# Splitting layer 1's first adaLN group around layer 0's experts, and writing a group's columns ahead of the gating

## The chip, the cores and the metric

The kernel runs on one core of a Trainium2 chip. What counts is the device time of one execution in microseconds (us); the kernel before took 1294.08 us, the median of three runs between 1293.26 and 1298.45.

## What is computed

One inference step of a four-layer diffusion backbone, float32 throughout: 128 context tokens and 256 latent tokens of width 1024 (384 columns together). Cut to what matters here:

```python
for i in range(4):                      # mixer: pool, mLSTM, MLA, pool
    mod = silu(cvec) @ w_ada[i] + b_ada[i]        # 6 x 1024 values, for each of two condition vectors
    h = rmsnorm(x, norm_mix[i]) * (1 + mod[1]) + mod[0]
    x = x + mod[2] * mixer(h)
    h = rmsnorm(x, norm_ffn[i]) * (1 + mod[4]) + mod[3]
    x = x + mod[5] * moe(h, ...)        # 16 experts of 256, two a token
```

w_ada of a layer is 1024 x 6144: 24 MB of weights for two vectors, so each byte is read once and used little. The experts of a layer are another 48 MB.

## The kernel before

**Weights.** All large weights go through `ring`, twelve SBUF slots of 1 MB (128 partitions x 2048 floats). `units` is the list of loads in order, written out by hand in a loop over the layers (L342 to L451); the SP queue walks it (`load`, L474). Unit u goes to slot u % 12, so SP first waits until unit u - 12 has been given back by its reader: each unit has a release (a semaphore and a value). SP is in order: a unit that waits holds back all behind it. A unit in `hold` also waits for a further event: the first unit behind a layer's expert weights waits until the last result gather (`yg_in[NT - 1]`) has landed, because the gathers would otherwise share the DMA engines with it.

**adaLN groups.** A layer's modulation comes in three groups of 2048 columns (shift and scale of the mixer; its gate and the experts' shift; the experts' scale and gate), numbered g = 3L, 3L+1, 3L+2. A group is eight units, one for 128 rows of w_ada. For some groups TensorE multiplies (`ada`, L543): for each row block four matmuls with a two-column stationary operand, 512 columns each, accumulated over the eight blocks in bank 7 (`ps[7]`). ScalarE copies the bank to `mrow` (`mod_rows`, L1302), TensorE turns it with four transposes into bank 7 again (`ada_columns`, L568), and VectorE adds the bias and writes the columns into `mod` (`mod_columns`, L1640). `ada_unit`, `ada_full`, `mrow_ready` and `mod_added` count these steps; bank 7 is one for all groups, so a group's first multiply waits until the columns of the one before are written. For others (4, 5, 8 to 11) VectorE accumulates the units (`mix`), and `ada_sum` only adds up partitions.

**Layer 0.** The units run: group 0, w_pool, groups 1 and 2, group 3 (which is layer 1's first), then 45 expert units; the sixteenth expert (12) goes to memory beside the ring (`load_side`). Group 3's blocks are multiplied by TensorE around the start of `experts(0, ...)`: four before it, 4 and 5 ahead of `count_picks`, 6 behind it, 7 behind the first `row_numbers`. Its row is copied and turned behind the first gate and up multiplies.

**Experts.** `experts(L, n)` (L1008) sorts token picks into ten rounds of 128 places, four tiles of 32 for an expert each. In a round TensorE does gates and ups (128 matmuls with 32-column stationary tiles), turns the next tokens, and does the downs of the round before (32 of 512 columns). POOL fetches rows of a round (`fetch`) and writes its results to DRAM (`store`); behind round 8's write it gathers each token's two result rows back, six gathers of 0.5 MB. Round 9's results go straight to `combine` (L1118): one matmul of 384 columns for each of the eight chunks, then 24 transposes that add the gathered rows, which ScalarE and VectorE have scaled and added. VectorE adds the outcome to xT, and the next layer's norm follows.

**mLSTM (layer 1).** In the value projection (12 outputs, c = 0 to 11) TensorE inserts `ada_sum(4)` at c = 3 and its transposes at c = 6; ScalarE copies the row at c = 4 and starts group 5's accumulators there (`mixed_first(5)`), for which VectorE's mix(5) waits. In the heads groups 6 and 7 are multiplied between the heads' matmuls: `ada_columns(6)` at head 2, and group 7's first two blocks behind head 2's fourth numerator. VectorE's order in head 2 is: states, `gated(1)`, `divided(2, 0)`, `weighted(3)`, `mod_columns(6)`, `carried(3)`, `divided(2, 1)`.

## Time and profile before

| | before |
|---|---|
| median of 3 runs | 1294.08 us |
| profiled execution, device time | 1297.72 us |
| its span | 1295.9 us |
| TensorE busy | 1170.8 us (90%) |
| VectorE busy | 582.6 us (45%) |
| ScalarE busy | 330.4 us (25%) |
| POOL busy | 123.3 us (10%) |
| DMA | 389.56 MB, 301 GB/s on the mean |
| mean granted TensorE clock | 0.956 |

The span is one execution as the hardware profiler saw it; the device time has a little around it. PE is TensorE's matmul, PEld its weight load, DVE VectorE, ACT ScalarE, SPq the queue of the SyncE engine, which issues the weight loads. All of TensorE's matmuls go through one helper (L531), so it is the tile names and shapes that tell them apart: `sb_ring,sb_cond` with 512 columns is an adaLN block, `sb_ring,sb_arena 128*32` an expert, `sb_arena 128*128 128x384` the start of combine, L1132 its transposes.

### The profile page before, as it was taken

The page shows a single profiled execution, that of the slowest core. Times are in us where ns is not written, and L with a number is a line of the kernel's source. Part 1 is how long each engine was busy: PE and PEld are TensorE (multiplying, and loading weights), DVE is VectorE, ACT ScalarE, POOL GpSimd, SP SyncE. Part 2 cuts the span into 40 slices and gives each one's busy share as a digit, 9 for nine tenths or more (in the row PEclk, how much of TensorE's full clock was granted, in tenths as well). Part 3 has the DMA queues.
Part 4 walks back from the last instruction along what each step waited for, and adds up shares of the span by engine and source line. Part 5 has one row for each costly group of instructions (what it writes and reads, how often), then busy time and mean ns, then how long its engine had stood idle before and what let it go on. Part 6 is the DMA issues. An engine that isn't in the chain of part 4 may idle for free.

```text
span 1295.9 us, 24580 instructions
## 1 busy us (share of the span) xinstructions
PE 1170.8 (90%) x10198; PEld 710.0 (55%) x10198; DVE 582.6 (45%) x1347; ACT 330.4 (25%) x724; POOL 123.3 (10%) x188
## 2 busy tenths in 40 slices
PE   4788998889999889799987999999799997799986
PEld 2346554346886545565545844555565545575544
DVE  1355211259651639731117876459741115741113
ACT  1240111241112640411115411340411114411113
POOL 2000110201000000011120000000011120011101
PEclk9898998989999999899999999899899998799998
DMA  9999999798774577398989973107489987578983
GB/s 354 406 422 419 417 406 421 292 386 321 263 283 161 207 268 307 132 373 345 387 325 356 395 281 129 53 1 276 163 326 356 411 336 296 225 297 339 385 369 138
DMA packets 89708, 389.56 MB, mean 301 GB/s; under 512 B 10456, under 2 KB 38604, under 8 KB 53240
## 3 DMA queue, kind: packets, MB, share of 16 engines
q1 hardware_dynamic: 71568, 336.61, 66.1%
q0 software_dynamic: 17456, 51.07, 10.9%
q8 instruction: 85, 1.39, 0.4%
q10 hardware_dynamic: 568, 0.23, 0.1%
q14 instruction: 31, 0.25, 0.1%
HBM read 370.96 MB, written 27.96 MB: 308 GB/s over the span
## 4 chain that ended last, share of the span: by engine, by line
PE 73%; DMA 11%; DVE 4%; ACT 3%; SPq 3%; issue 3%; POOL 1%; POOLq 0%; DVEq 0%; ACTq 0%
PE bank L531 67%; DMA sb_ring<-in_w_ada 3%; PE bank L1081 3%; SPq L489 3%; DMA sb_ring<-in_w_exp_down 2%; DMA slot_out<-sb_arena,sb_homes 2%; DMA sb_arena<-slot_out,sb_slots 2%; DMA token_rows<-sb_arena 1%; POOL sb_arena L2354 1%; PE bank L1099 1%; DVE sb_xT L2207 1%; DVE sb_hT L1687 1%; PE bank L1030 1%; DMA sb_arena<-token_rows,sb_rows 1%; ACT sb_hT L1353 1%
## 5 line engine op out<-in xcount | busy, mean ns | idle before, releaser
L531 PE MATMUL bank<-sb_ring,sb_arena 128*32 128x256 f32 (+1 forms) x6112 | 456.8, 430 | 19.4 <-DMA sb_ring<-in_w_exp_down 6.0
L531 PEld LDWEIGHTS bank<-sb_ring,sb_arena 128*32 128x32 f32 x6112 | 227.1, 112 | 190.9 <-issue 113.0
L531 PE MATMUL bank<-sb_arena 128*128 128x128 f32 (+11 forms) x776 | 137.0, 354 | 9.0 <-ACT sb_arena L1513 2.3
L531 PE MATMUL bank<-sb_ring,sb_hT 128*128 128x256 f32 x624 | 141.3, 388 | 4.2 <-ACT sb_hT L1343 4.2
L1677 DVE SCALAR_TENSOR_TENSOR sb_arena<-sb_ring,sb_cond,sb_arena 128x2048 f32<-128x2048 f32 (+1 forms) x70 | 139.1, 2024 | 11.9 <-ACT sb_scratch L1313 11.7
L531 PEld LDWEIGHTS bank<-sb_ring,sb_hT 128*128 128x128 f32 x624 | 120.2, 194 | 25.8 <-issue 8.7
L2154 DVE TENSOR_TENSOR sb_arena<-sb_arena,bank 128x256 f32<-128x256 f32 x40 | 16.8, 421 | 259.0 <-PE bank L531 259.0
L531 PEld LDWEIGHTS bank<-sb_arena 128*128 128x128 f32 (+2 forms) x776 | 99.2, 188 | 43.5 <-issue 21.7
L531 PE MATMUL bank<-sb_arena,sb_ring 128*128 128x384 f32 (+2 forms) x288 | 93.9, 501 | 0.0
L531 PE MATMUL bank<-sb_hT,sb_ring 128*128 128x384 f32 x256 | 86.3, 500 | 2.6 <-ACT sb_hT L1343 2.6
L2161 DVE COPY sb_arena<-bank 128x512 f32<-128x512 f32 x40 | 27.7, 692 | 130.9 <-PE bank L531 130.9
L531 PEld LDWEIGHTS bank<-sb_arena,sb_ring 128*128 128x128 f32 (+1 forms) x288 | 49.1, 178 | 41.4 <-issue 15.9
L531 PEld LDWEIGHTS bank<-sb_hT,sb_ring 128*128 128x128 f32 x256 | 49.9, 196 | 38.2 <-issue 5.2
L1534 ACT ACTIVATE sb_arena<-bank 128x512 f32<-128x512 f32 x40 | 23.9, 598 | 153.6 <-PE bank L1081 135.7
L531 PE MATMUL bank<-sb_ring,sb_cond 128*2 128x512 f32 x384 | 50.5, 653 | 11.6 <-DMA sb_ring<-in_w_ada 7.6
L1323 ACT ACTIVATE sb_scratch<-sb_xT 128x768 f32<-128x768 f32 (+1 forms) x45 | 31.5, 715 | 107.7 <-DVE sb_xT L1704 97.9
L1538 ACT ACTIVATE sb_arena<-bank 128x256 f32<-128x256 f32 x40 | 15.4, 386 | 166.2 <-PE bank L531 166.2
L1687 DVE SCALAR_TENSOR_TENSOR sb_hT<-sb_xT,sb_amp,sb_rstd 128x128 f32<-128x128 f32 (+1 forms) x128 | 43.1, 412 | 12.7 <-ACT sb_rstd L1336 12.6
L2333 POOL DMA_INDIRECT slot_out<-sb_arena,sb_homes x27 | 27.1, 1005 | 226.4 <-DVE sb_arena L2161 223.2
L2322 POOL DMA_INDIRECT sb_arena<-token_rows,sb_rows x36 | 36.8, 1021 | 122.2 <-DVE sb_slots L2189 73.5
L1550 ACT ACTIVATE sb_arena<-bank 128x512 f32<-128x512 f32 x40 | 23.9, 598 | 80.8 <-PE bank L531 80.8
L2313 POOL DMA_DIRECT2D token_rows<-sb_arena x12 | 6.6, 548 | 386.8 <-ACT sb_arena L1513 386.7
(343 smaller groups left out, 1168.2 us busy)
## 6 DMA issues: line engine op xcount, KB each, us to landing
sb_ring<-in_w_ada SPq DMA_DIRECT2D x96, 1024.0 KB
sb_ring<-in_w_exp_gate SPq DMA_DIRECT2D x60, 1024.0 KB
sb_ring<-in_w_exp_up SPq DMA_DIRECT2D x60, 1024.0 KB
sb_ring<-in_w_exp_down SPq DMA_DIRECT2D x60, 1024.0 KB
sb_ring<-in_w_mlstm_in SPq DMA_DIRECT2D x12, 1024.0 KB
token_rows<-sb_arena POOLq DMA_DIRECT2D x12, 512.0 KB, 3.9
slot_out<-sb_arena POOLq DMA_DIRECT2D x9, 512.0 KB, 9.1
sb_scratch<-in_w_exp_gate SPq DMA_DIRECT2D x4, 1024.0 KB
```

The source lines that it names most:

```text
L489: sp.dma_start(slot(u)[:, 0:n].rearrange("p (k n) -> p k n", k=k), ap).then_inc(slot_in[u % RING], 16)
L531: return pe.matmul(out, lhsT, rhs, start=first, stop=last)
L1081: ins = pe.transpose(ps[2 + c][:, k * P:(k + 1) * P], xg[:, (o - 1) % 2, (4 * c + k) * P:(4 * c + k + 1) * P], ident[:, :])
L1323: act.activation(sq[:, a:b, :], xT[:, a:b, :], ACT.Square).then_inc(sq_ready, 1)
L1534: act.activation(xgT[:, o % 2, 0:4, :].rearrange("p k s -> p (k s)"), ps[2][:, :], ACT.Copy).then_inc(xa_ready, 1)
L1550: act.activation(ysb[:, o % 2, 0:512], ps[5][:, :], ACT.Copy).then_inc(ya_ready, 1)
L1677: ins = v.scalar_tensor_tensor(out=ap, in0=w[:, a:b], scalar=cond[:, k, c:c + 1], in1=ap, op0=ALU.mult, op1=ALU.add)
L1687: v.scalar_tensor_tensor(out=hT[:, k, a:b], in0=xT[:, k, a:b], scalar=gain[:, k, c:c + 1], in1=rstd[:, a:b], op0=ALU.mult, op1=ALU.mult).t ...
L2154: v.tensor_tensor(hid[:, :].rearrange("p (j q) -> p j q", j=2), sil[:, :].rearrange("p (q j) -> p j q", j=2), ps[1][:, 0:FE].rearrange("p ...
L2161: v.tensor_copy(ysb[:, o % 2, 512:1024], ps[6][:, :]).then_inc(yb_ready, 1)
L2322: g.indirect_dma_start(out=xg[:, (o - 1) % 2, :], out_offset=None, in_=Xg, in_offset=bass.IndirectOffsetOnAxis(ap=rows[:, o:o + 1], axis=0 ...
L2333: g.indirect_dma_start(out=Yg, out_offset=bass.IndirectOffsetOnAxis(ap=homes[:, o:o + 1], axis=0), in_=ysb[:, o % 2, :], in_offset=None, b ...
```

## The change

Group 3 is cut into two halves of four units. The first half stays where it is in the list; the second comes behind layer 0's last expert unit, and the held unit is the one behind it. TensorE multiplies blocks 0 to 3 before the experts; that half's row is copied, turned and written to `mod` with the bias (semaphore `half_done`). Blocks 4 to 7 are multiplied between round 9's downs and `combine`, as an accumulation of their own in bank 7. combine's chunk 5, which uses bank 7, waits for ScalarE's copy. The second half is turned behind layer 1's first norm and added to what `mod` holds. In the mLSTM layer, group 4's sum, copy, transposes and the start of group 5 move up by one or two outputs, and `mod_columns(6)` moves ahead of `gated(1)`.

```diff
-        def ada_units(*groups):
+        def ada_units(*groups, rows=range(KC)):
...
-                for k in range(KC):
+                for k in rows:
...
-        ADA_WINDOW = [(3,), (), (), ()]
+        SPLIT = 3
...
-            ada_units(*ADA_WINDOW[L])
+            if L == 0:
+                ada_units(SPLIT, rows=range(4))
             moe_first.append(len(units))
 
-            hold[len(units) + 3 * (NE - 1)] = (yg_in[NT - 1], 32 * (L + 1))
+            hold[len(units) + 3 * (NE - 1) + (4 if L == 0 else 0)] = (yg_in[NT - 1], 32 * (L + 1))
...
             assert len(units) == moe_first[L] + 3 * (NE - 1)
+            if L == 0:
+                ada_units(SPLIT, rows=range(4, KC))
...
+                                 k == 0 or g == SPLIT and k == 4, k == KC - 1 or g == SPLIT and k == 3)
...
-                        if c == 3:
+                        if c == 2:
                             ada_sum(4)
-                        if c == 6:
+                        if c == 4:
                             ada_columns(4)
...
-                for g in ADA_WINDOW[L]:
-                    ada(g, 4, 5)
                 if L == 0:
                     count_picks()
-                for g in ADA_WINDOW[L]:
-                    ada(g, 6)
...
                 row_numbers(ps[4], 0, 3, 6 * L + 2)
-                for g in ADA_WINDOW[L]:
-                    ada(g, 7)
...
+                        if L == 0 and c == 5:
+                            pe.wait_ge(mrow_ready, SPLIT + 1)
                         mm(bank[c][:, 0:TOK], ysb[:, (ROUNDS - 1) % 2, c * P:(c + 1) * P], last_a, True, False)
...
                 gates_ups(0)
-                for g in ADA_WINDOW[L] + ADA_OUTPUT[L]:
+                for g in ADA_OUTPUT[L]:
                     ada_columns(g)
+                if L == 0:
+                    pe.wait_ge(half_done, 1)
+                    turn_rows().then_inc(half_done, 1)
                 tokens(1)
...
                 down(ROUNDS - 1)
                 state["u"] += 3 * (NE - 1)
+                if L == 0:
+                    pe.wait_ge(slots_ready, 6)
+                    ada(SPLIT, 4, 5, 6, 7)
                 combine()
...
                     norm(2 * L)
+                if L == 1:
+                    ada_columns(SPLIT)
...
-                for g in ADA_WINDOW[L]:
-                    ada(g, 0, 1, 2, 3)
+                    ada(SPLIT, 0, 1, 2, 3)
                 experts(L, 2 * L + 1)
...   ScalarE
-                    if c == 4:
+                    if c == 2:
                         mod_rows(4)
                         mixed_first(5)
...
+                if L == 0:
+                    act.wait_ge(ada_unit, 8 * SPLIT + 4)
+                    act.wait_ge(ada_full, SPLIT)
+                    act.activation(mrow[:, :], ps[7][:, :], ACT.Copy).then_inc(half_done, 1)
                 silu(0)
...
                 out(ROUNDS - 1)
+                if L == 0:
+                    act.wait_ge(half_done, 2)
+                    mod_rows(SPLIT)
                 for t in range(NT):
                     scale(t)
...   VectorE
+            def half_columns():
+                v.wait_ge(half_done, 2)
+                bias_columns(SPLIT, mod[:, 1, 0:16, :].rearrange("p (q j) c -> p q j c", q=4),
+                             ps[7][:, :].rearrange("p (j q c) -> p q j c", j=4, q=4)[:, :, :, 0:2]).then_inc(half_done, 1)
...
+                if n == SPLIT:
+                    v.wait_ge(half_done, 3)
+                    v.tensor_tensor(out, cols, out, ALU.add).then_inc(mod_added, 1)
+                else:
+                    bias_columns(n, out, cols).then_inc(mod_added, 1)
...
                     states(h)
+                    if h == 2:
+                        mod_columns(ADA_MIXER[1][0])
                     if h:
                         gated(h - 1)
                     divided(h, 0)
                     if h + 1 < MH:
                         weighted(h + 1)
-                    if h == 2:
-                        mod_columns(ADA_MIXER[1][0])
...
                 kind = L % 3
+                if L == 1:
+                    mod_columns(SPLIT)
                 norm(2 * L, amp[:, L, 0, :, :])
```

## Rows read from the trace of the kernel before

**Rows 1.** The page: the span, and DMA's busy tenths in 40 slices.
```profile
span 1295.9 us, 24580 instructions
...
DMA  9999999798774577398989973107489987578983
```

**Rows 2.** Windows: length, busy us of each engine (instructions), clock, DMA share, GB/s.
```profile
87.40:240.70 153.30, 140.92 (x1829) 78.63 (x1833) 41.70 (x155) 26.03 (x54) 16.05 (x21) 0.96 1.01 416
...
162.00:163.00 1.00, 1.00 (x28) 0.57 (x23) 0.00 (x0) 0.00 (x0) 0.69 (x2) 1.00 0.87 320
...
240.70:244.70 4.00, 1.60 (x18) 0.43 (x10) 0.42 (x1) 0.39 (x1) 1.66 (x2) 0.90 0.19 44
...
244.00:247.30 3.30, 3.28 (x16) 0.89 (x20) 0.00 (x0) 0.00 (x0) 2.60 (x3) 0.50 0.76 216
...
244.70:254.20 9.50, 9.50 (x48) 4.07 (x41) 2.13 (x3) 2.90 (x3) 4.37 (x5) 0.86 0.87 299
```

**Rows 3.** Timeline of SP's weight issues: start, length from first to last, count.
```profile
115.29 0.35 SPq L489 DMA_DIRECT2D sb_ring<-in_w_exp_gate  x1
127.08 0.34 SPq L489 DMA_DIRECT2D sb_ring<-in_w_exp_up  x1
...
140.71 3.79 SPq L489 DMA_DIRECT2D sb_ring<-in_w_exp_up  x2
...
150.39 10.71 SPq L489 DMA_DIRECT2D sb_ring<-in_w_exp_down  x2
...
255.47 1.01 SPq L489 DMA_DIRECT2D sb_ring<-in_w_mlstm_in  x2
```

**Rows 4.** Timeline of TensorE, layer 0: start, length, what, [idle before, releaser].
```profile
71.67 5.33 PE L531 MATMUL bank<-sb_ring,sb_cond 128*2 128x512 f32 x48
...
87.44 1.04 PE L531 MATMUL bank<-sb_ring,sb_cond 128*2 128x512 f32 x8 [1.27 <-DMA sb_ring<-in_w_ada]
...
120.25 1.25 PE L1081 MATMUL bank<-sb_ident,sb_arena 128*128 128x128 f32 x8 [1.92 <-DMA sb_arena<-token_rows,sb_rows]
...
201.25 6.17 PE L531 MATMUL bank<-sb_ring,sb_arena 128*32 128x256 f32 x64 [4.16 <-DMA sb_ring<-in_w_exp_gate]
...
244.02 5.26 PE L531 MATMUL bank<-sb_ring,sb_arena 128*32 128x512 f32 x32 [1.80 <-DMA sb_ring<-in_w_exp_down]
249.21 5.43 PE L531 MATMUL bank<-sb_arena 128*128 128x384 f32 x16
...
257.06 4.29 PE L1132 MATMUL bank<-sb_ident,sb_arena 128*128 128x128 f32 x22 [1.35 <-DVE sb_arena L2167]
```

**Rows 5.** POOL's timeline; landing of the three token writes (by tile token_rows, 88:125).
```profile
233.74 0.53 POOL L2331 DMA_DIRECT2D slot_out<-sb_arena  x1 [2.88 <-DVE sb_arena L2161]
...
249.30 0.99 POOL L2354 DMA_INDIRECT sb_arena<-slot_out,sb_slots  x1 [0.30 <-issue]
...
DMA to landing us min/median/max: 8.9/11.6/14.3
```

**Rows 6.** Timelines of TensorE and VectorE in mLSTM's heads, and one window.
```profile
447.67 1.03 PE L531 MATMUL bank<-sb_arena,sb_hT 128*128 128x257 f32 x4
...
453.18 3.60 PE L531 MATMUL bank<-sb_ring,sb_cond 128*2 128x512 f32 x16 [3.61 <-issue]
456.70 2.08 PE L531 MATMUL bank<-sb_arena,sb_hT 128*128 128x257 f32 x4
...
447.26 1.23 DVE L1847 TENSOR_TENSOR sb_arena<-sb_arena,sb_scratch 128x256 f32<-128x256 f32 x3 [0.60 <-ACT sb_scratch L1445]
...
452.89 0.18 DVE L1645 TENSOR_TENSOR sb_mod<-bank,sb_b_ada 128x32 f32<-128x32 f32 x1
...
453.20:458.50 5.30, 5.30 (x20) 1.89 (x21) 0.09 (x1) 0.00 (x0) 0.00 (x0) 0.50 0.46 138
```

**Rows 7.** Value projection of mLSTM: VectorE's wait ahead of group 5, TensorE beside it.
```profile
341.88 1.28 DVE L1677 SCALAR_TENSOR_TENSOR sb_arena<-sb_ring,sb_cond,sb_arena 128x1024 f32<-128x1024 f32 x1 [11.65 <-ACT sb_scratch L1313]
...
345.86 27.79 PE L531 MATMUL bank<-sb_ring,sb_hT 128*128 128x256 f32 x128
```

More of the change, by code:

```diff
@@ L305, in build @@
         yt_ready = sem("yt_ready"); yd_ready = sem("yd_ready"); out_y = sem("out_y")
+        half_done = sem("half_done")
         NCONST, NMLA = 8, 12
@@ L552, in ada @@
                     for q in range(4):
-                        ins = mm(ps[7][32 * q:32 * q + 2, :], cond[:, k, :], w[:, q * 512:(q + 1) * 512], k == 0, k == KC - 1)
+                        ins = mm(ps[7][32 * q:32 * q + 2, :], cond[:, k, :], w[:, q * 512:(q + 1) * 512],
+                                 k == 0 or g == SPLIT and k == 4, k == KC - 1 or g == SPLIT and k == 3)
                     ins.then_inc(ada_unit, 1)
@@ L566, in ada_sum, with turn_rows @@
                 ins.then_inc(ada_unit, KC)
+            def turn_rows():
+                for j in range(4):
+                    ins = pe.transpose(ps[7][:, j * P:(j + 1) * P], mrow[:, j * P:(j + 1) * P], ident[:, :])
+                return ins
             def ada_columns(g):
                 pe.wait_ge(mrow_ready, g + 1)
-                for j in range(4):
-                    ins = pe.transpose(ps[7][:, j * P:(j + 1) * P], mrow[:, j * P:(j + 1) * P], ident[:, :])
-                ins.then_inc(ada_full, 1)
+                turn_rows().then_inc(ada_full, 1)
             def norm_squares(n, a, b):
@@ L1143, in experts @@
                     if o == 1:
-                        for g in ADA_WINDOW[L] + ADA_OUTPUT[L]:
+                        for g in ADA_OUTPUT[L]:
                             pe.wait_ge(mod_added, g + 1)
+                        if L == 0:
+                            pe.wait_ge(half_done, 3)
                         turn_last()
@@ L1557, in experts @@
                 tokens(0)
-                for g in ADA_WINDOW[L] + ADA_OUTPUT[L]:
+                for g in ADA_OUTPUT[L]:
                     mod_rows(g)
+                if L == 0:
+                    act.wait_ge(ada_unit, 8 * SPLIT + 4)
+                    act.wait_ge(ada_full, SPLIT)
+                    act.activation(mrow[:, :], ps[7][:, :], ACT.Copy).then_inc(half_done, 1)
                 silu(0)
@@ L1572, in experts @@
                 out(ROUNDS - 1)
+                if L == 0:
+                    act.wait_ge(half_done, 2)
+                    mod_rows(SPLIT)
                 for t in range(NT):
@@ L1638, in _, with bias_columns @@
                 v.tensor_copy(xT[:, c, :], ps[c % 4][:, 0:TOK]).then_inc(x_ready, 1)
+            def bias_columns(n, out, cols):
+                return v.tensor_tensor(out, cols, b_ada[:, 16 * n:16 * (n + 1)].rearrange("p (q j) -> p q j", q=4)
+                                       .unsqueeze(3).to_broadcast([P, 4, 4, 2]), ALU.add)
+            def half_columns():
+                v.wait_ge(half_done, 2)
+                bias_columns(SPLIT, mod[:, 1, 0:16, :].rearrange("p (q j) c -> p q j c", q=4),
+                             ps[7][:, :].rearrange("p (j q c) -> p q j c", j=4, q=4)[:, :, :, 0:2]).then_inc(half_done, 1)
             def mod_columns(n):
@@ L1644, in mod_columns @@
                 cols = ps[7][:, :].rearrange("p (j q c) -> p q j c", j=4, q=4)[:, :, :, 0:2]
-                v.tensor_tensor(mod[:, L, 16 * g:16 * (g + 1), :].rearrange("p (q j) c -> p q j c", q=4), cols,
-                                b_ada[:, 48 * L + 16 * g:48 * L + 16 * (g + 1)].rearrange("p (q j) -> p q j", q=4)
-                                .unsqueeze(3).to_broadcast([P, 4, 4, 2]), ALU.add).then_inc(mod_added, 1)
+                out = mod[:, L, 16 * g:16 * (g + 1), :].rearrange("p (q j) c -> p q j c", q=4)
+                if n == SPLIT:
[3 more added lines that the diff above has]
+                    bias_columns(n, out, cols).then_inc(mod_added, 1)
                 v.wait_ge(mod_added, n + 1)
@@ L2172, in experts @@
                 rows_and_columns(at, 3, COLS)
-                for g in ADA_WINDOW[L] + ADA_OUTPUT[L]:
+                for g in ADA_OUTPUT[L]:
                     mod_columns(g)
+                if L == 0:
+                    half_columns()
                 for o in range(1, ROUNDS - 1):
```

## The prediction

> **What bounds the kernel now.** I read the page's slices first: the DMA row stands at 9 for seven slices of 32.4 us, then at 7 in the eighth (227 to 259 us), where layer 0 ends [rows 1]. The windows say how full the pipe is: 416 GB/s from 87.4 to 240.7 us, almost nothing (44 GB/s) for the next four microseconds, then 299 GB/s while the six result gathers run [rows 2]. So layer 0's experts look like a stage that the weight stream bounds, with idle DMA at its end. Two further views qualify that. The DMA queue's issues show when the ring of 12 slots lets SP go on [rows 3]: most expert weights are issued the moment TensorE gives a slot back. TensorE's own timeline [rows 4] shows that it waits for weights only in the last third: 4.2 us at 201.25 and 1.8 us at 244.02; of the 153.3 us of the full stream it is busy for 140.9 [rows 2]. The reader is to see that the stream is long behind early and late, and almost dry in the middle: at 162 us the pipe moved only 320 GB/s [rows 2].
>
> **Four weights leave the front of the stream.** A ring unit is 1.05 MB, so 2.52 us at 416 GB/s; four are 10.1 us. That is the most that the last expert weight can gain. The ring decides how much is left of it. Before, the fourth adaLN unit lands at 87.44 [rows 4]. After it, in the changed order, come thirteen expert units that need no late release (the last is the one issued at 115.29), with POOL's three token writes and two fetches of 0.52 MB each: 16.3 MB, 39 us, done about 126.5. The next unit cannot be issued before 127.08, when expert 1's gate weight is released by TensorE, whose own time has not changed. Three units and a fetch are then through by about 137.5, and the next waits for 140.71. So the stream starves twice where it did not before; the two gaps with some 1.5 us of start-up each take about 8 of the 10 us. The unit behind 150.39 (the second one, issued at its end, 161.1) meets an empty queue: landed about 165.6. Ten more (four gates and ups, a down, three of the side expert, two gates) and 2.9 MB of POOL's make 13.4 MB, 32.2 us: 197.8, where the wait at 201.25 ended before. Lead left: 3.4 us, bounded by 0 and 10. I take 3.4, since the rows of issue give it.
>
> TensorE follows: its stall before 201.25 shrinks from 4.2 to 0.8 us, and the expert rounds end about 3 us earlier. The last expert weight lands near 240.6 instead of 244.0. The four blocks of adaLN multiplies taken out ahead of the experts stood in waits for VectorE, except the last (0.9 us), behind which the next tokens wait for a fetch to land at 120.25 anyway [rows 4]: worth 0 to 0.9, I take 0. The half row that is copied and turned there replaces a full one of the same size: 0.
>
> **What they cost behind.** The write of round 8's rows is issued 3 us earlier than 233.74, and the six gathers (1.3 us apart, the last issued at 249.30) likewise, from about 239.7 [rows 5]. Now the stream is not silent: 4.2 MB follow the last expert weight. How the two queues share is read from the three token writes in the full stream: issued a microsecond apart, landed 8.9, 11.6 and 14.3 us after issue, so 3.7 us apart, 0.142 MB/us, a third of the pipe [rows 5]. The ring keeps 0.275 MB/us: 0.33 MB until 241.5, then 3.86 MB in 14.0 us: the last adaLN unit lands at 255.5. The gathers have 1.17 MB left then, 2.8 us: 258.3 instead of 255.4 (before, the held mLSTM weight, which waits for them, is issued at 255.47 [rows 3]).
>
> TensorE's queue is the dearer side. The four adaLN blocks stand in front of combine(), so its sixteen 384-column multiplies, 5.43 us, which before ran at 249.21 in the shadow of the gathers [rows 4], wait for that last unit. One block costs 0.89 us at full clock (5.33/6), double at half; TensorE has sat idle for most of 3.8 us, and after such idling the granted clock is 0.50 for 3.3 us [rows 2]. So 1.8 us in the block, then 5.43 plus 0.75 for the 1.5 us that still run at half: 263.5. The result transposes begin there and not at 257.06: **+6.4 us** (between -1.2 with the full lead, and about +12 with none). ScalarE's copy of the row and its scaling stand beside the multiplies and end about 261. Queued behind the new wait on TensorE is everything up to layer 1's first norm.
>
> At layer 1's start the second half is turned and added after the norm's mean, before the scaling of the inputs: four transposes (0.6) and two small VectorE additions beside ScalarE's two rstd steps: +0.2 (0 to 0.6).
>
> **The step ahead of the gating.** In the heads TensorE stops from 449.57 to 453.18, then runs the two adaLN blocks in 3.60 and four more multiplies in 2.08 at clock 0.50 [rows 6]. What it waits for is the columns of group 6, since they free the bank: VectorE idles 0.60 us ahead of the gating at 447.26, but writes them at 452.89, behind the gating, the division and the next weighting. Moved ahead, they are done by 447.1, before TensorE arrives. Gone are 3.61 us, 3.60 less 1.78 at full clock = 1.82, and 2.08 less 1.03 = 1.05: 6.5; ScalarE's next copies and head chain follow with a little less, so **-6.3 us** (-3.6 to -6.5). The gating itself waits for ScalarE until 447.26 and loses nothing. What is late next is ScalarE's square-and-exp chain, which moves with it. The columns of group 4 one step earlier spare VectorE most of an 11.65 us wait, but TensorE runs 27.79 us unbroken beside it, and VectorE ends in time there already [rows 7]: 0 (up to 0.5 either way).
>
> **Sum:** +6.4 + 0.2 - 6.3 = +0.3. The profiled execution took 1297.7 us (span 1295.9), 3.6 above the median; the sum is a difference and is laid on the median: 1294.4.
>
> **Rivals.**
> The whole lead arrives. If the stream does not starve, because the slots come free sooner than I read, the last weight lands at 234, TensorE is its own limit (experts end 11 us earlier, and the gathers start 7.6 us earlier), the last adaLN unit lands at 247.9, transposes at 255.9: -1.2 + 0.2 - 6.3, 1286.8. For it: the DMA row of 9s. Against: the dip to 320 GB/s at 162 while the stream was 10 us further behind.
>
> Equal shares at the end. If gathers and ring halve the pipe, the gathers are through at 256.6 and the ring at 258.3, and the combine waits 2.8 us longer: 1297.2. For it: both sides have work on all engines. Against: the token writes took a third. The Trainium skill, "DMA: Bandwidth & Descriptors", section "Queues, rings and completion order", says that each engine takes the queues in turn, packet by packet; by that rule this rival's shares would hold, while the trace's 3.7 us per half megabyte shows a third.
>
> The heads don't move. If the idle at 449.57 is another wait (the view calls it "issue"), -6.3 falls away: 1300.7. Against: the wait's end at 453.18 sits 0.1 us behind the columns' write.
>
> Slower: no lead, and the combine behind the stream. Place: TensorE's queue ahead of combine(). If the starved stream's restarts eat all 10 us, the last adaLN unit lands 3.4 us later than in my sum, and 1.5 us more for each restart that 161 us no longer absorbs, two of them: at 262. The transposes start 12.9 us late: 12.9 + 0.2 - 6.3 = +6.8, 1300.9. It decides from a last landing past 261.7. For it: three dry spots, each with a restart. Against: at 161 us the stream of before still had a unit or two queued, which the changed one gains.
>
> **How the numbers follow.** My forecast 0.50 (its own range 1291 to 1298), whole lead 0.20, equal shares 0.12, heads unmoved 0.08, slower 0.10. A measurement here tells 0.5% (6.5 us) from nothing, so faster means below 1287.6 and slower above 1300.6. Faster: the whole-lead case, 0.20. Slower: the last case and a quarter of the unmoved heads, 0.12. Same: 0.68. The range takes in both outer cases nearly whole: 1286 to 1301.5.
>
> **What would show it.** Right: GB/s well under 400 somewhere in 127 to 129 and 137 to 142 us, TensorE's wait near 201 under 1.5 us, the last adaLN block near 255, transposes of the result near 263, no TensorE gap between the heads' blocks and the mLSTM stage 6 us shorter from its first multiply to its last. Wrong: no dips and a last expert weight before 237 (then faster), or the gathers landed by 255 and the combine already done; a gap of 3 us left in the heads would refute that term.

## Result and the profile after

| | before | after |
|---|---|---|
| median | 1294.79 us (1291.24 to 1304.22, 15 runs) | 1299.63 us (1293.41 to 1307.93, 15 runs) |
| ratio, 95% interval | 1 | 1.0044 [1.0023, 1.0065] |
| profiled execution | 1297.72 us | 1306.47 us |
| its span, granted clock | 1295.9 us, 0.956 | 1304.6 us, 0.946 |

The forecast was 1294.4 us, range 1286 to 1301.5: the range holds the time, the likeliest case misses it by 5.2 us. A second measurement, told below as a control, gave 1.0074 [1.0046, 1.0102]; weighted together the two say 1.0055, some 7 us. So the change makes the kernel slower, by about what a measurement can tell. The executions of after scatter over 14.5 us, and the profiled one lies near the upper end, so what follows reads stages and not ends. One execution of a later kernel (d2) took 2510.9 us, nearly twice the others; the median doesn't feel it.

**The stream's front.** Windows of the kernel after, over the stretch in which the four weights are gone, and over the end (length, busy us of each engine, clock, DMA share, GB/s):

```profile
87.40:125.00 37.60, 27.62 (x278) 22.32 (x281) 23.96 (x116) 9.33 (x20) 3.71 (x5) 0.84 1.01 418
125.00:165.00 40.00, 40.00 (x557) 21.20 (x553) 8.06 (x23) 5.89 (x12) 4.84 (x6) 0.98 0.80 298
165.00:200.00 35.00, 34.19 (x482) 16.96 (x470) 5.42 (x9) 5.90 (x12) 4.26 (x5) 1.00 1.01 408
...
245.00:250.00 5.00, 4.29 (x25) 1.44 (x29) 0.00 (x0) 0.60 (x1) 3.42 (x4) 0.66 1.01 421
250.00:255.00 5.00, 2.77 (x28) 0.64 (x20) 0.69 (x1) 0.00 (x0) 2.62 (x3) 1.00 1.02 413
255.00:260.00 5.00, 2.25 (x16) 0.21 (x16) 0.00 (x0) 0.00 (x0) 0.00 (x0) 0.66 0.94 374
260.00:265.00 5.00, 5.00 (x14) 2.53 (x11) 2.47 (x3) 4.14 (x6) 0.00 (x0) 0.66 0.19 55
```

The same two middle windows of the kernel before:

```profile
125.00:165.00 40.00, 40.00 (x577) 21.32 (x572) 6.59 (x15) 6.17 (x13) 5.84 (x7) 1.00 1.01 413
165.00:200.00 35.00, 32.09 (x442) 15.70 (x434) 5.41 (x9) 5.63 (x12) 4.84 (x6) 0.99 1.01 412
```

The reader is to see 298 against 413 GB/s over 40 us: 4.6 MB less, and four ring units are 4.2 MB. Everything that was taken out of the front is missing by 165 us, and nothing is left over as a lead. SP's issues of after (start, length, count) say why, beside [rows 3]:

```profile
116.35 0.35 SPq L494 DMA_DIRECT2D sb_ring<-in_w_exp_gate  x1
129.18 0.34 SPq L494 DMA_DIRECT2D sb_ring<-in_w_exp_up  x1
142.81 3.79 SPq L494 DMA_DIRECT2D sb_ring<-in_w_exp_up  x2
152.89 10.30 SPq L494 DMA_DIRECT2D sb_ring<-in_w_exp_down  x2
218.89 12.18 SPq L494 DMA_DIRECT2D sb_ring<-in_w_ada  x4
263.55 1.00 SPq L494 DMA_DIRECT2D sb_ring<-in_w_mlstm_in  x2
```

The releases by TensorE pace the queue, and each comes 1.1 to 2.5 us later than before: the one at 161.1 now at 163.2. So TensorE's releases pace the stream there with or without the four weights: in the kernel before the pipe runs low by itself, 320 GB/s at 162 us.

**TensorE in layer 0 of after** (start, length, what, [idle before, releaser]), to be laid beside [rows 4]:

```profile
97.20 0.66 PE L536 MATMUL bank<-sb_arena,sb_ones 128*128 128x48 f32 x2 [3.09 <-DVE sb_arena L2047]
...
102.30 8.80 PE L536 MATMUL bank<-sb_arena 128*128 128x128 f32 x60 [2.78 <-DVE sb_arena L2080]
...
122.20 1.09 PE L1084 MATMUL bank<-sb_ident,sb_arena 128*128 128x128 f32 x8 [2.81 <-DMA sb_arena<-token_rows,sb_rows]
...
202.91 10.30 PE L536 MATMUL bank<-sb_ring,sb_arena 128*32 128x256 f32 x128 [3.72 <-DMA sb_ring<-in_w_exp_gate]
...
245.71 5.34 PE L536 MATMUL bank<-sb_ring,sb_arena 128*32 128x512 f32 x32 [1.82 <-DMA sb_ring<-in_w_exp_down]
250.84 1.93 PE L536 MATMUL bank<-sb_ring,sb_cond 128*2 128x512 f32 x16
255.15 1.04 PE L536 MATMUL bank<-sb_ring,sb_cond 128*2 128x512 f32 x8 [2.38 <-DMA sb_ring<-in_w_ada]
258.79 1.88 PE L536 MATMUL bank<-sb_ring,sb_cond 128*2 128x512 f32 x8 [2.59 <-DMA sb_ring<-in_w_ada]
260.60 6.81 PE L536 MATMUL bank<-sb_arena 128*128 128x384 f32 x16
267.24 2.78 PE L1137 MATMUL bank<-sb_ident,sb_arena 128*128 128x128 f32 x24
```

The wait near 201 is still 3.7 us long, the last expert weight is 1.7 us later than at 244.02, and the transposes begin 10.2 us later than at 257.06. Ahead of the counts (97.20) TensorE has idled 3.09 us where the blocks stood, and runs the next matmuls at half clock. Two windows of after show it:

```profile
93.80:97.00 3.20, 0.31 (x3) 0.07 (x1) 2.96 (x16) 2.98 (x5) 1.62 (x3) 0.87 1.02 425
97.00:100.00 3.00, 2.31 (x10) 2.21 (x10) 0.48 (x4) 0.00 (x0) 0.00 (x0) 0.50 1.00 416
```

In the kernel before the same 97 to 100 us had a clock of 1.00:

```profile
97.00:100.00 3.00, 2.26 (x18) 1.30 (x18) 1.41 (x11) 0.00 (x0) 0.00 (x0) 1.00 1.00 401
```

**ScalarE and VectorE at layer 0's end**, after:

```profile
260.79 0.60 ACT L1320 ACTIVATE sb_mrow<-bank 128x512 f32<-128x512 f32 x1 [11.36 <-PE bank L536]
261.28 3.56 ACT L1569 ACTIVATE sb_arena<-sb_arena 128x1024 f32<-128x1024 f32 x4
...
267.77 5.29 DVE L2242 SCALAR_TENSOR_TENSOR sb_xT<-bank,sb_mod,sb_xT 128x128 f32<-128x128 f32 x16 [1.44 <-PE bank L1137]
...
277.34 5.36 DVE L1720 SCALAR_TENSOR_TENSOR sb_hT<-sb_xT,sb_amp,sb_rstd 128x128 f32<-128x128 f32 x16 [0.40 <-ACT sb_rstd L1350]
```

A queue that the prediction did not price: the gathered rows' scaling stands behind the copy of adaLN's row on ScalarE, so it too waits 11.4 us for the stream. At layer 1's start the norm's scaling still waits 0.40 us for rstd behind the two small additions: they cost little: from the transposes to the first mLSTM matmul it takes 11.54 us, before 11.45.

**The heads of after**, beside [rows 6]:

```profile
454.91 0.60 PE L536 MATMUL bank<-sb_arena,sb_hT 128*128 128x257 f32 x2
455.43 1.90 PE L536 MATMUL bank<-sb_ring,sb_cond 128*2 128x512 f32 x16
457.26 1.14 PE L536 MATMUL bank<-sb_arena,sb_hT 128*128 128x257 f32 x4
```

The gap of 3.61 us is gone and the block is at full clock.

### The profile page after: what moved, and what is told of

It is laid out like the page before. It is cut to its first block, busy times and chain, and to the rows that moved or that the text cites. A ratio compares the mean times of both kernels' runs of the same rounds, so it can differ in the third digit from the quotient of the medians.

```text
span 1304.6 us, 24594 instructions
## 1 busy us (share of the span) xinstructions
PE 1177.7 (90%) x10202; PEld 717.1 (55%) x10202; DVE 582.9 (45%) x1348; ACT 329.8 (25%) x725; POOL 123.4 (9%) x188
## 4 chain that ended last, share of the span: by engine, by line
PE 73%; DMA 13%; DVE 5%; ACT 3%; SPq 2%; issue 2%; POOL 1%; POOLq 0%; DVEq 0%; ACTq 0%
PE bank L536 67%; DMA sb_ring<-in_w_ada 5%; PE bank L1084 3%; SPq L494 2%; DMA sb_ring<-in_w_exp_down 2%; DMA sb_arena<-token_rows,sb_rows 2%; DMA slot_out<-sb_arena,sb_homes 2%; DMA sb_arena<-slot_out,sb_slots 1%; PE bank L1102 1%; DVE sb_hT L1720 1%; PE bank L1137 1%; PE bank L1039 1%; POOL sb_arena L2391 1%; ACT sb_hT L1367 1%; DVE sb_xT L2242 1%
## 5 line engine op out<-in xcount | busy, mean ns | idle before, releaser
L536 PE MATMUL bank<-sb_arena 128*128 128x128 f32 (+11 forms) x776 | 142.7, 364 | 10.0 <-DVE sb_arena L2080 2.8
L536 PEld LDWEIGHTS bank<-sb_arena 128*128 128x128 f32 (+2 forms) x776 | 103.9, 196 | 45.3 <-issue 22.9
L536 PE MATMUL bank<-sb_hT,sb_ring 128*128 128x384 f32 x256 | 83.5, 488 | 2.3 <-ACT sb_hT L1357 2.3
L2359 POOL DMA_INDIRECT sb_arena<-token_rows,sb_rows x36 | 36.9, 1024 | 127.4 <-DVE sb_slots L2224 74.4
```

The source lines that it names most:

```text
L536: return pe.matmul(out, lhsT, rhs, start=first, stop=last)
L2359: g.indirect_dma_start(out=xg[:, (o - 1) % 2, :], out_offset=None, in_=Xg, in_offset=bass.IndirectOffsetOnAxis(ap=rows[:, o:o + 1], axis=0 ...
```

## Experiments

Eleven kernels ran, each against the kernel before on the same chip, twelve times each (c4 six times). The table reads four lengths from TensorE's timeline of each profile; they start and end inside a stage, so that most of what differs between executions drops out. G: from the router's first matmul (88.30 in the kernel before, 88.94 after) to the second gates and ups (122.34 and 124.12). R: from there to the downs of the last expert weight (244.02, 245.71). B: from there to layer 1's first value projection (319.12, 326.60). H: from the adaLN block that stands at 436.17 in the kernel before to the one at 470.72. In c4 and c3 H is 1.7 us longer, since the clock is at 0.50 for two to three microseconds around head 2's start.

| kernel | ratio [95%] | median us | G | R | B | H |
|---|---|---|---|---|---|---|
| before | 1 | 1290.5 to 1297.2 | 34.0 | 121.7 | 75.1 | 34.55 |
| after | 1.0044 [1.0023, 1.0065] | 1299.63 | 35.2 | 121.6 | 80.9 | 28.0 |
| c4, after again | 1.0074 [1.0046, 1.0102] | 1300.80 | 34.9 | 122.7 | 80.1 | 29.7 |
| e1, columns of 6 only | 0.9959 [0.9933, 0.9985] | 1291.60 | 34.1 | 121.3 | 73.0 | 28.0 |
| c1, both steps only | 0.9962 [0.9936, 0.9987] | 1288.01 | 34.1 | 120.4 | 74.9 | 28.0 |
| e2, split only | 1.0076 [1.0048, 1.0105] | 1303.88 | 35.9 | 122.2 | 80.2 | 34.65 |
| e3, nothing behind | 0.9981 [0.9955, 1.0007] | 1293.45 | 35.3 | 121.4 | 73.8 | 28.0 |
| e4, zeros in front | 1.0018 [0.9989, 1.0048] | 1299.49 | 32.9 | 121.4 | 82.7 | 28.0 |
| c2, combine first | 1.0018 [0.9992, 1.0044] | 1292.41 | 35.1 | 121.6 | 79.0 | 28.0 |
| c3, c2 with zeros | 1.0038 [1.0011, 1.0066] | 1296.79 | 34.1 | 122.0 | 79.4 | 29.7 |
| d1, two behind | 0.9972 [0.9942, 1.0003] | 1288.58 | 33.9 | 121.3 | 76.1 | 28.0 |
| d2, d1 combine first | 0.9989 [0.9953, 1.0024] | 1294.39 | 33.9 | 122.0 | 79.0 | 28.0 |
| d3, e3 with zeros | 0.9975 [0.9943, 1.0006] | 1288.46 | 34.2 | 122.4 | 74.4 | 28.0 |

The three kernels with an untouched layer 0 (before, e1, c1) have G at 34.1, R at 121.1 and B at 74.3 on the mean, with spreads of 0.1, 1.3 and 2.1. G holds the router's own sixteen matmuls, which took 1.4 to 2.45 us by the clock that they met. From their end the untouched kernels take 32.0 us on the mean, the five in which TensorE idles ahead of the counts 33.3, the three with zeros 31.7: the same order as in G.

**e1: the columns alone.**

```diff
                     states(h)
+                    if h == 2:
+                        mod_columns(ADA_MIXER[1][0])
                     if h:
                         gated(h - 1)
```

> The kernel before with one edit: the columns of group 6 are written ahead of the gating. Theory A (TensorE's 3.6 us stop in head 2 waits for those columns, and the half clock behind it comes from the stop): 5.5 to 8 us faster, ratio 0.994 to 0.996, no stop longer than 1 us ahead of group 7's first block, which then takes 1.9 us and not 3.6. Rival B (the stop moves to another wait, the chain of square and exp on ScalarE): within 2 us of before, a new wait of 2 to 4 us within head 2 or 3.

Measured -5.3 us [-8.7, -1.9], and H shorter by 6.5 us. The term stands.

**e2: the split alone**, without the two steps in the mLSTM layer.

```diff
-                        if c == 2:
+                        if c == 3:
                             ada_sum(4)
```

> The changed kernel without the two steps of the mLSTM layer (columns ahead of the gating, group 4 one output earlier): the split of group 3 alone. Theory A (the split costs what its trace shows by the result's transposes, 267.24 against 257.06, less what a warmer start of layer 1 returns): 9 to 13 us slower than before, ratio 1.007 to 1.010. Rival B (the split is near nothing and the steps are what cost, by group 4's sum waiting on TensorE): ratio 0.998 to 1.002.

Measured +9.9 us [+6.2, +13.6]; e1 and e2 add to +4.6, the whole change measured +5.7 [+3.0, +8.4]. No interplay of the parts shows, as far as intervals of 3 to 4 us either way can tell, and the split is the loss.

**e3: no second half.** Blocks 4 to 7 and their weights are left out; one block of zeros stands for them.

```diff
-            if L == 0:
-                ada_units(SPLIT, rows=range(4, KC))
...
-                    ada(SPLIT, 4, 5, 6, 7)
+                    for q in range(4):
+                        ins = mm(ps[7][32 * q:32 * q + 2, :], order[:, 0:2], mrow[:, :], True, True)
```

> The changed kernel with the second half of group 3 left out (four 1 MB loads and their multiplies; one block of zeros stands in, so layer 1's shift and scale miss half of their sum). It shows what the front alone gains. Theory A (ring slots, not bytes, pace the middle of layer 0; the front is even late because TensorE is cold): last expert weight lands within 1.5 us of where the changed kernel has it (245.7), transposes of the result at 257 to 260, so the front brings nothing; against before -3 to -8 us in all, by the steps. Rival C (four units less bring their 10 us once nothing is loaded behind): last expert weight before 240 and -12 us or more.

Window and last expert weight of this kernel:

```profile
125.00:165.00 40.00, 40.00 (x565) 21.23 (x561) 7.38 (x20) 5.89 (x12) 5.64 (x7) 0.99 0.82 302
```

```profile
244.84 5.34 PE L534 MATMUL bank<-sb_ring,sb_arena 128*32 128x512 f32 x32 [1.80 <-DMA sb_ring<-in_w_exp_down]
```

A stream with four weights less, and nothing behind it, takes 121.4 us from the second gates to the last expert weight, like the untouched ones (120.4 to 121.7). There is no lead to begin with. B is that of the untouched kernels: all of the tail's price comes from what stands behind the experts. By time the kernel is 2.5 us faster than before [-5.8, +0.9], a little less than the 3 to 8 expected.

**e4: TensorE kept busy in front**, zeros multiplied where blocks 4, 5 and 6 stood, the rest as after.

```diff
+                    nothing(2, False)
                     count_picks()
+                    nothing(1, True).then_inc(ada_unit, 1)
```

> The changed kernel with blocks of zeros multiplied where the before kernel had adaLN blocks 4, 5 and 6 (two blocks ahead of the pick counts, one behind): same results, TensorE not idle there. Theory A (3.1 us of idle ahead of the counts drop the clock to half, which makes the counts and the first gather matmuls late by 1.2 us and layer 0's rounds by 1.8): count matmuls at full clock, second round's gates at about 122.3 instead of 124.1, whole kernel 1 to 2 us faster than the changed one. Rival D (the fetch's landing sets the second round, not TensorE): gates still at 124, nothing gained.

```profile
96.14 0.42 PE L536 MATMUL bank<-sb_arena,sb_ones 128*128 128x48 f32 x2 [1.27 <-DVE sb_arena L2055]
96.40 0.60 PE L536 MATMUL bank<-sb_arena,sb_tri 128*128 128x16 f32 x4
```

The counts are at full clock and G is 2.3 us shorter, 0.3 of it in the router's matmuls; the ratio fell by 0.0026, which the intervals do not resolve. Over the profiles, G is 35.3 on the mean where TensorE idles (after, c4, e2, e3, c2), 33.7 with zeros (e4, c3, d3), and 34.1 in the untouched kernels: the idle start costs 1.2 us, and zeros give it back. R does not answer: 121.9 on the mean of the eight kernels with four weights gone. The gain reaches the first mLSTM matmul: 187.65 us behind the router's first in e4, 189.84 in after. Behind it most is lost again, in the same sixteen matmuls at a lower clock (0.76 over this stretch in e4, 1.00 in after), e4 first:

```profile
275.83 7.12 PE L536 MATMUL bank<-sb_hT,sb_ring 128*128 128x384 f32 x16 [2.28 <-ACT sb_hT L1365]
```

```profile
278.78 5.66 PE L536 MATMUL bank<-sb_hT,sb_ring 128*128 128x384 f32 x16 [2.28 <-ACT sb_hT L1357]
```

That is 1.5 of the 1.8 us by which B is longer.

**c1: both steps, no split.**

```diff
-                        if c == 3:
+                        if c == 2:
                             ada_sum(4)
```

> The kernel before with both steps of the mLSTM layer and no split: the columns of group 6 ahead of the gating, and group 4's sum, copy, transposes and the start of group 5 one or two outputs earlier. Theory (group 4's step is worth nothing, since TensorE runs 27.79 us unbroken beside VectorE's wait): the same as the columns of group 6 alone, which measured 0.9959, so 1291.5 and a ratio of 0.995 to 0.997; the mLSTM value projection's matmuls stay back to back and VectorE's 11.65 us wait shrinks without moving anything. Rival (the earlier bank-7 work gets in TensorE's way, or the earlier sum waits for group 4's last unit): 1 to 3 us slower than the columns alone, a gap of TensorE at outputs 2 to 4. Rival on the other side: VectorE's group 5 does end late somewhere, and 1 to 2 us more are gained.

Measured -4.9 us [-8.3, -1.7], like e1. From the first value projection to the last block of them it takes 67.2 us in before, e1, after and c1 alike. Group 4's step is worth nothing.

**c2: seven of combine's eight matmuls ahead of the adaLN blocks.**

```diff
-                    for c in (1, 2, 3, 0, 4, 5, 6, 7):
+                    for c in (1, 2, 3, 0, 4, 6, 7, 5):
...
                         if L == 0 and c == 5:
+                            pe.wait_ge(slots_ready, 6)
+                            ada(SPLIT, 4, 5, 6, 7)
                             pe.wait_ge(mrow_ready, SPLIT + 1)
```

> The changed kernel, but seven of combine's eight start matmuls (the ones that do not use bank 7) stand ahead of the four adaLN blocks behind the experts; the eighth follows the row's copy. In the changed kernel the last block came at 258.79, the start of combine took 6.81 us from 260.60, and the transposes began at 267.24. Theory (TensorE's order is what turns the late stream into a late stage): the last block stays near 258.8, behind it come the row's copy (about 1 us) and one matmul of 384 columns, transposes near 262.8, so 4 to 4.5 us earlier, the first mLSTM matmul near 274.4 instead of 278.78; 1295 to 1296, ratio about 1.001. Rival (the gathers and their scaling are what the transposes wait for, not the multiplies): they start at 265 or later with a wait on ScalarE or VectorE, and at most 2 us are gained, ratio 1.003. Rival (the seven multiplies ahead of the blocks let TensorE's clock fall further behind them): last blocks at half clock, no gain.

```profile
257.72 1.04 PE L536 MATMUL bank<-sb_ring,sb_cond 128*2 128x512 f32 x8 [1.02 <-DMA sb_ring<-in_w_ada]
...
263.91 4.96 PE L1139 MATMUL bank<-sb_ident,sb_arena 128*128 128x128 f32 x22 [0.28 <-DVE sb_arena L2199]
```

```profile
258.88 0.60 ACT L1319 ACTIVATE sb_mrow<-bank 128x512 f32<-128x512 f32 x1 [10.64 <-PE bank L536]
259.37 2.17 ACT L1568 ACTIVATE sb_arena<-sb_arena 128x1024 f32<-128x1024 f32 x2
262.28 1.33 ACT L1568 ACTIVATE sb_arena<-sb_arena 128x512 f32<-128x512 f32 x2 [0.74 <-DMA sb_arena<-slot_out,sb_slots]
```

VectorE's update of xT begins at 264.44 instead of 267.77, 3.3 us earlier, and the first mLSTM matmul 3.35. Against after on the same chip (c4) the kernel is faster by 0.6% (0.2 to 0.9), against the first measurement of after the intervals overlap. B is only 1.9 us shorter than in after, since the first mLSTM matmuls run at a lower clock here too (7.09 us against 5.66). Both the theory and the rival were half right: TensorE's order is one bound; a microsecond or two behind it stands the next, the gathers, whose last landing ScalarE waits for at 262.28.

**c3: c2 and the zeros of e4.**

```diff
+                    nothing(2, False)
                     count_picks()
...
+                            ada(SPLIT, 4, 5, 6, 7)
```

> As the run with seven of combine's matmuls first, and with three blocks of multiplies by zeros where blocks 4 to 6 of group 3 stood ahead of the experts (in the changed kernel alone these gave back the full clock and started the tokens 3.1 us earlier). Theory (cold start and combine's order are separate terms and add): counts at full clock near 96.1, tokens near 119.1, second gates near 121.1, last adaLN block near 256.2, transposes near 260.2, first mLSTM matmul near 272: 3 us less than without the zeros, 1292 to 1293, ratio 0.998 to 0.999; still not below the columns of group 6 alone (0.996), since the split then still costs about 3 us against 257.06. Rival (the lead that the warm start leaves arrives whole once nothing waits behind it): transposes near 258 and a ratio of 0.995 or less. Rival (what is given back at the front is eaten by the starved stream again): transposes at 262 or later and the same ratio as without the zeros.

The expectation missed: 1.0038, not under c2. In this profile G is 1.0 us shorter than in c2 and gives back 0.4 in R, B is not shorter, and H, the same code, is 1.7 us longer by half clock. The clock had also fallen by the end of the counts (0.89 over their first 1.4 us), so the zeros did not hold it as in e4. The transposes begin at 263.00, 174.7 us behind the router's first matmul against 174.9 in c2, which is what the last rival expected. The two terms are too small to be told from the clock's scatter by time.

**c4: the changed kernel once more**, as a control beside c1 to c3.

> The changed kernel once more, beside the others on one chip: ratio 1.0044 again within its interval (1.002 to 1.007), transposes near 267, counts at half clock. If it comes out at 1.001 or less, the differences between chips are as large as the terms that the other runs are to tell apart, and only traces can.

1.0074, its interval overlapping the first; transposes at 268.96, 20.8 us behind the last expert weight. TensorE idles 3.09 us ahead of the counts here too, but the clock falls only 1.4 us behind their start.

**d1: two units behind, not four.** Blocks 4 and 5 are multiplied where they stood before.

```diff
-                ada_units(SPLIT, rows=range(4))
+                ada_units(SPLIT, rows=range(6))
...
-                    ada(SPLIT, 4, 5, 6, 7)
+                    ada(SPLIT, 6, 7)
```

> The changed kernel with two units of group 3 behind the experts instead of four; blocks 4 and 5 are multiplied ahead of the counts, where they stood before. Theory (the tail's price is the time by which the stream outlasts the gathers; nothing of the lead arrives): the counts run at full clock, so TensorE gives back 1.6 us in front of the last expert weight; behind it the last block, which in the changed kernel waited 13.1 us from the last expert weight with the last two waits 3.64 us apart, waits about 6 us and so hides in the downs; the gathers land 5 us earlier than 17.8 us behind the last expert weight, the transposes come about 14.2 us behind it (changed kernel 21.5, before 13.0). Against the changed kernel -7.3 and -1.6, against the kernel before +1.2 and -6.5: ratio 0.996 (0.994 to 0.999). Rival (the price goes by the unit: each unit behind the experts costs a quarter of the changed kernel's 8.4 us): +4.2 - 6.5 and -1.6 at most: ratio 0.998 to 1.000, transposes near 17 us behind the last expert weight. Rival (part of the lead of a half as large starved stretch does arrive): the last expert weight over 1.5 us earlier than in the kernel before against the router's matmuls (155.2 us there), ratio 0.994 or less.

```profile
125.00:165.00 40.00, 40.00 (x577) 21.31 (x573) 6.60 (x15) 5.92 (x13) 5.85 (x7) 1.00 0.94 360
```

```profile
243.58 5.34 PE L536 MATMUL bank<-sb_ring,sb_arena 128*32 128x512 f32 x32 [1.83 <-DMA sb_ring<-in_w_exp_down]
248.70 1.93 PE L536 MATMUL bank<-sb_ring,sb_cond 128*2 128x512 f32 x16
250.56 5.43 PE L536 MATMUL bank<-sb_arena 128*128 128x384 f32 x16
...
257.65 2.62 PE L1138 MATMUL bank<-sb_ident,sb_arena 128*128 128x128 f32 x22 [1.24 <-DVE sb_arena L2201]
```

The stream misses 2.1 MB (53 GB/s less over 40 us): exactly the two units, so again no lead. The transposes stand 14.1 us behind the last expert weight (forecast 14.2; after 21.5, before 13.0). The price is not by the unit (17 us was expected for that); it fits the time by which the stream outlasts the downs and the gathers. The ratio, 0.9972, is the steps' gain with about a microsecond lost.

**d2: d1 with c2's order.**

```diff
-                    for c in (1, 2, 3, 0, 4, 5, 6, 7):
+                    for c in (1, 2, 3, 0, 4, 6, 7, 5):
...
+                            ada(SPLIT, 6, 7)
```

> As the run with two units behind, and seven of combine's start matmuls ahead of their two blocks. Theory (with two units the stream ends before the gathers, so the order no longer matters): the same within 1 us, transposes 14 us behind the last expert weight, ratio 0.996. Rival (the price goes by the unit and by TensorE's order): 2 us less than the run with two behind alone.

```profile
256.45 0.60 ACT L1320 ACTIVATE sb_mrow<-bank 128x512 f32<-128x512 f32 x1 [8.00 <-PE bank L536]
256.94 3.40 ACT L1569 ACTIVATE sb_arena<-sb_arena 128x1024 f32<-128x1024 f32 x4
```

Both theories missed. The weights had landed, but the blocks now stand behind seven matmuls, the row's copy comes at 256.45 instead of 250.74, and the scaling behind it on ScalarE slips from 251.23 to 256.94. B grows by 2.9 us, the first mLSTM matmul is 3.6 us later against the router's. The same edit that gains 3.3 us with four units loses 3.6 with two.

**d3: e3 with zeros in front** (half of the sum left out, as in e3).

```diff
-                ada_units(SPLIT, rows=range(4, KC))
...
+                    nothing(2, False)
                     count_picks()
```

> Half of group 3 left out altogether (so half of that sum is missing), with three blocks of multiplies by zeros where blocks 4 to 6 stood and both steps of the mLSTM layer. Theory (the front's shortened stream brings no lead; what the missing blocks cost was TensorE's clock): the last expert weight at or at most 1 us ahead of the kernel before (155.2 us behind the router's matmuls), TensorE's wait ahead of it 1.8 us as before, first mLSTM matmul within 1 us of the kernel before, ratio 0.995 (only the 6.5 us of the heads). Rival (a lead of 3.4 us as my sum had it): last expert weight near 151.8, ratio 0.992.

R is 122.4: no lead here either, with the counts at full clock. The last expert weight comes 156.7 us behind the router's first matmul, 1.5 later than the theory's 155.2, and the first mLSTM matmul 180.55 (before 180.21). 0.9975 [0.9943, 1.0006] is some 3 of the steps' 5 us, its interval taking in all of them. The rival expectation, a lead of 3.4 us, is refuted.

## Why the prediction was right in its range and wrong in its sum

Lengths from the last expert weight and from the router's matmuls give each term its own size.

| step | forecast | measured |
|---|---|---|
| TensorE's start without the blocks (G) | 0 | +1.2 (five kernels, 35.3 less 34.1) |
| lead at the last expert weight (R) | -3.4 | none; +0.8 (eight kernels, 121.9 less 121.1, spreads of 1.3) |
| transposes behind the last expert weight, against 13.04 | +9.8 | +8.5 (21.5 less 13.0; +8.2 on the means of after, c4, e2 and of the untouched) |
| layer 1's start: columns | +0.2 | +0.1; but 2.3 us come back behind it, the first mLSTM matmuls being at full clock in after, c4 and e2 |
| columns of group 6 | -6.3 | -6.5 in H, -5.3 by time |
| group 4's step | 0 | 0 |
| sum | +0.3 | +1.9 in the traces (G, R and B of after, c4 and e2 +8.4, H -6.5), +5.7 and +9.5 by time |

**The step that failed is the lead.** I let the changed stream's unit of 161 us land at 165.6, added 32.2 us of load and got 197.8, "where the wait at 201.25 ended before". The two sides were not of one kind, a modelled time after against a measured one before. The same sum holds for the kernel before, word for word: its unit was issued at 161.1 too, into a pipe that moved 320 GB/s at that moment [rows 2, 3]. It gives 197.8 there as well, 3.4 us short of what the trace has. The 3.4 us were my sum's own error. The rows had the answer: at 161 us the stream of before had run down to the pace of TensorE's releases, so no unit that is taken out ahead of it can be felt behind it. Two windows refute the lead (298 against 413 GB/s, then 408 against 412), R in e3 and d3 with nothing behind, and d1's 360 GB/s with half the dose.

**TensorE's blocks in front** I took as worth 0, bounded by 0 and a gain of 0.9. They were worth having: without them TensorE idles 3.09 us instead of 1.26, works at half clock behind it, and sends tokens, second gates and every release after them 1.2 us late. The first link can be read directly: the sixty matmuls behind the counts begin 11.65 us behind the router's end in after, e2 and e3, where the counts ran at 0.50, and 10.62 in the kernel before. The bound was one-sided, since I priced only the work that went, not the clock that it held.

**The tail** came near in its sizes: from the last expert weight to the last wait for an adaLN unit 13.1 us (forecast 14.9), to the landed gathers 17.8 (forecast 17.7), the combine in TensorE's queue behind it. The way there was not the one forecast, so the agreement is in part luck. The first gather was issued with the last expert weight and not 0.9 us ahead of it, since round 8's write took 9.7 us to land beside the stream (before 8.5). From 245.71 to 250 us SP's queue had the pipe to itself (1.75 MB, the gathers' 0.01), and 1.2 of the four units' 4.2 MB had gone through ahead of 245.71. Only then did the two share. The queues' packets, MB and busy share (q1 is SP's, q0 POOL's), first in after from 250 to 254 us, then under the token writes of before, 98 to 108 us:

```profile
q1 hardware_dynamic: 137, 0.97, 58.6%
q0 software_dynamic: 187, 0.68, 43.2%
```

```profile
q1 hardware_dynamic: 387, 2.82, 66.8%
q0 software_dynamic: 381, 1.43, 34.9%
```

The third that I took from the token writes is right for them; beside the gathers POOL's queue had 41% of the bytes. The equal-shares rival is refuted in its landing (its ring is done 17.7 us behind the last expert weight, the trace's 13.1), but for the share itself the truth lay between. The Trainium skill, "DMA: Bandwidth & Descriptors", section "Queues, rings and completion order", has the engines take the queues in turn, a packet at a time. Under the token writes the trace agrees, 387 packets to 381; but SP's carried 7.3 KB on the mean and POOL's 3.8. So I read the rule wrongly when I said that by it the rival's equal shares would hold: equal turns gave a third of the bytes. What I missed is that ScalarE's scaling queues behind the same stream; with TensorE's order alone it did not matter, with that order mended (c2, d2) it does.

**The heads** came out to 0.2 us: the wait was VectorE's order, as [rows 6] showed.

**The rivals.** That the range holds the time is not the sum's merit: the range was drawn to take in the outer rivals. The slower one, no lead with the combine behind the stream, is nearest to what happened: 1300.9 against 1299.6 measured. It erred in the landing, which it put at 262 and the trace has no later than 258.8, and I had given it 0.10 on the ground that at 161 us the stream still had a unit queued. Whole lead and unmoved heads are refuted.

**What stays open.** The traces' sum of +1.9 us is under the measured +5.7 [+3.0, +8.4]. It leaves out the stretch between B and H, 115.5 us in after, c4, e2 and e1 against 117.0 in before and c1, by the clock over the heads' first adaLN block; with it the sum is +0.9. From the heads' last adaLN block to the end, where all kernels have the same code, the profiles take 822 to 835 us, the clock being different in each; one profile a kernel can't say whether the change has a share in that. Of e2 (+8.8 in G, R and B, +9.9 by time) little is left over, of e1 (-6.5, -5.3) a microsecond. So the rest is either scatter or a lower clock later on. The executions of c4 had a mean granted clock of 0.945, those of before beside them 0.953, which fits a cost but doesn't place it.

## What to carry to other kernels

Before a modelled time is set against a measured one, run the same sum on the kernel before: if it misses the trace there, the difference is the sum's error, not the change's gain. Work taken out of a prefetch stream is felt only up to the next place where the reader's releases already pace it; look for dips in GB/s and for issues that wait for a release. Here everything taken out ahead of them was worth nothing. When a late arrival is put at the end of a stage, list what queues behind its wait on every engine in it, and the clock that removed filler had kept up.

The best version here is the step in the heads alone: 0.9959 [0.9933, 0.9985], with group 4's step 0.9962; the intervals of d1, d3 and e3 overlap theirs.

## What the runs showed of the hardware

- An idle time of 3.09 us ahead of the counts was followed at once by a granted clock of 0.50 in after, e2 and e3, of 0.72 over the next 1.4 us in c2, and of 1.00 for 1.4 us and 0.56 behind in c4: the same gap, a different moment of the fall. With 1.27 us in e4 it stayed at 1.00 over the counts, with 1.25 in c3 it was 0.89 over their first 1.4 us and 0.50 behind. Some 3 us of zeros (1.90 and 1.04 in e4) gave 1.5 us back at the second gates (G, means of three and five kernels).
- Two DMA queues with work at once moved equal packets and unequal bytes: 387 to 381 packets, 2.82 to 1.43 MB, over 10 us of before. 0.5 MB gathers issued 1.3 us apart from 245.67 on moved only 0.01 MB until 250.
- The executions of before spread over 12 to 19 us in a measurement. Among the 35 of one, the span falls by 11 us for each 0.01 of mean granted clock (correlation -0.81), among the 29 of each of two others by 7 (-0.84) and 9 (-0.94): differences under 0.3% come out only in many runs or in single stages.
- The clock also falls at places that no edit touched and ahead of which TensorE hardly idled: in c3 and c4 to 0.50 in the heads, behind 0.76 us of idle time; the heads' first adaLN block took 5.31 us in before, 3.62 in e1 and 5.18 in c1.
